# Up projection of the last feed-forward by a seven-product 2x2 scheme, on one Trainium2 core

## The chip, the core and the metric

One program runs on one core of a Trainium2 chip. The metric is the device time of one execution in microseconds. The kernel before takes 1809.07 us (median of 3 runs, 1808.6 to 1810.55). Engines are named as in the profile: PE is TensorE's matmul, PEld its weight load, DVE is VectorE, ACT is ScalarE, POOL is GpSimd, SP is SyncE, which issues most transfers.

## What is computed

A stream of 512 tokens with 1024 channels passes through two layers, each a SwiGLU feed-forward, a token mixer (Fourier, then convolution) and a second SwiGLU feed-forward, all modulated by a conditioning vector. The change lies in the last feed-forward alone:

```python
def swiglu(h, w_in, w_out):
    g, u = jnp.split(h @ w_in, 2, axis=-1)
    return (jax.nn.silu(g) * u) @ w_out
...
h = h + 0.5 * m[8] * swiglu(modulate(rms_norm(h), m[6], m[7]), w_ff_in[i, 1], w_ff_out[i, 1])
```

Here `w_in` is 1024 x 5632 and `w_out` 2816 x 1024, in fp32.

## The kernel before

Everything is kept with channels on the 128 partitions and the 512 tokens along the free axis. A product in fp32 is made of three matmuls on operands split in two: each operand is written as a rounded part (`_hi`) plus a remainder (`_lo`), and `product` (L1488) adds hi x hi, lo x hi and hi x lo in one PSUM bank. ACT makes every `_hi` by a copy into the rounded type, and DVE makes every `_lo` by subtracting it from the full value.

A feed-forward `f` goes through `NI = 11` steps. A step takes 256 gate columns and 256 up columns of `w_in`, that is two chunks `ch` of 128 gate and 128 up channels. For each chunk `up` (L1594) runs 8 blocks of input channels x 2 (gate, up) x 3 matmuls of 512 tokens into banks `ps[2*ch]` (gate) and `ps[2*ch+1]` (up). ACT takes the SiLU of the gate bank into `tmp_a` (`silu`, L779), DVE multiplies it with the up bank into `tmp_b` (`gate_product`, L1138), ACT and DVE split the result into `p_hi` and `p_lo` (L784, L1143). `down` (L1602) multiplies the step's two product chunks with 256 rows of `w_out` for 8 output chunks `d`, 6 matmuls each, in banks 4 to 7 in turn, and DVE adds each to the stream `h` (`flush`, L1148), times a gate. The down product of step `i - 1` runs behind the up products of step `i`:

```python
def step(i, par):
    up(f, i, 0)
    up(f, i, 1)
    down(f, i - 1, 1 - par)
```

Step 0 is `first_two` (L1533), which works on halves of 256 tokens while the normalised input is still being made. Steps 1 to 10 have the form above: step 1 by itself, 2 to 9 as a loop of four rounds of two steps (`LOOP_STEPS`, L68), 10 by itself. After step 10 the last down product (48 matmuls) runs and the output is stored.

Weights come in by SP: a pair (gate and up columns of one step, 2 MB, one of two buffers `raw_pair`) and a down block (1 MB, `raw_down`). ACT and DVE convert a chunk's pair in one instruction each of 128x2048 elements (`next_hi` L788, `next_lo` L1161), the down block likewise (L653, `down_lo` L985), into three weight buffers `w_hi`/`w_lo`, two for the up chunks and one for down. SP's `ff_step` (L465) waits until the second chunk of the pair two steps back is converted, loads the next pair into its place, then waits until the down block is converted and loads the next. Each engine's instructions run in the order in which they are written out, per engine, for each step: DVE's `ff_step` (L1165) does the down weights, the first chunk's product, its next weights, the second chunk's product, the eight flushes and the second chunk's next weights. Semaphore counts in the loops are computed from the loop register.

Before the last feed-forward, the norm (number 6) fills `a_hi` and `a_lo` half by half: DVE scales `h` into a temporary (`half_tmp`, L248, tiles of `tmp_b` and `tmp_c`), ACT adds the shift and rounds (`half_hi`, L708), DVE takes the remainder (`half_lo`, L1076). `y_conv` (L219) is a view of `raw_mod`, which is not used any more by then. POOL has no work in the last feed-forward.

Of the kernel before, what the change touches and what calls it, by code (L numbers as in the profile page):

```python
# [39 lines left out]
def hybrid_backbone(nc, x_chunks, c, w_mod, w_mod_first, w_ff_in, w_ff_out, fnet_w_out, conv_w_in, conv_w_out,  # L40
# [125 lines left out]
    with ctx:  # L166
# [229 lines left out]
        def _(sp):  # L396
# [90 lines left out]
            def feed_forward(f, next_pairs):  # L487
# [27 lines left out]
                with sp.Fori(0, LOOP_STEPS[f]) as r:  # L515
                    for odd in range(2):
                        step(r * 2 + (1 + odd), odd, f < 3)
                for i in range(1 + 2 * LOOP_STEPS[f], NI - 2):
                    step(i, (i - 1) % 2, i < UNIT_STEPS[f])
# [1430 lines left out]
```

## Time and profile before

| | us |
|---|---|
| median of 3 runs | 1809.07 |
| lowest, highest | 1808.6, 1810.55 |
| the profiled execution | 1811.04 |
| its span, first to last instruction | 1809.3 |
| PE busy | 1774.1 (98%) |
| DVE busy | 1112.4 (61%) |
| ACT busy | 600.8 (33%) |
| POOL busy | 170.9 (9%) |

The mean granted clock of TensorE is 0.991 of 2.4 GHz. A line of the page such as `L1579 PE MATMUL bank<-a_hi,w_hi 128*128 128x512 f32 x1408` names the line of the kernel, the engine, the tiles and the shape. "Busy" of one instruction runs from its start to its end, and on every engine the next instruction may start before that end, so that the distance between starts (here called the pitch) is read from the timeline. Steps 1 to 10 of the last feed-forward lie at 1468.46 to 1794.86 us of the span.

### The profile page before, as it was taken

What the parts mean: (1) busy time and instruction counts of PE and PEld (TensorE: products, weight loads), DVE (VectorE), ACT (ScalarE), POOL (GpSimd) and SP (SyncE); (2) the same over time, 40 slices, a digit from 0 to 9 for tenths busy, and PEclk for the clock granted to TensorE, in tenths of its full rate; (3) what the DMA queues carried; (4) which work ended last, traced back from release to release, by engine and by line L of the source; (5) the groups of instructions that cost most, each with busy time, mean ns of one, the idle gap of its engine ahead of it and who ended that gap; (6) DMA issues with size and microseconds to landing.
All of it is one profiled execution on the core that took longest, in us unless ns stands there. A gap on an engine that the chain in (4) does not pass through costs nothing.

```text
span 1809.3 us, 21295 instructions
## 1 busy us (share of the span) xinstructions
PE 1774.1 (98%) x8424; PEld 1470.6 (81%) x8424; DVE 1112.4 (61%) x1448; ACT 600.8 (33%) x761; POOL 170.9 (9%) x146
## 2 busy tenths in 40 slices
PE   7999999999999999999999999999999999999999
PEld 5788888889888888888988888888765888888887
DVE  5865665667766656566656556456898555444454
ACT  5422222235342222223422222226676442222221
POOL 0000000020300000001000000004994200000000
PEclk8999999999999999999999999999999999999999
DMA  9744353330633534534343535221211322423301
GB/s 370 285 159 190 116 205 143 142 137 1 227 145 116 216 132 150 198 116 148 108 165 144 204 116 183 72 70 48 93 48 47 117 71 70 139 70 104 105 23 70
DMA packets 133375, 238.07 MB, mean 132 GB/s; under 512 B 3777, under 2 KB 110401, under 8 KB 124738
## 3 DMA queue, kind: packets, MB, share of 16 engines
q1 hardware_dynamic: 133168, 236.99, 36.5%
q8 instruction: 42, 0.69, 0.2%
q10 hardware_dynamic: 146, 0.24, 0.0%
q14 instruction: 19, 0.16, 0.0%
HBM read 235.12 MB, written 2.10 MB: 131 GB/s over the span
## 4 chain that ended last, share of the span: by engine, by line
PE 88%; DVE 4%; POOL 4%; ACT 2%; issue 1%; DMA 0%; POOLq 0%; ACTq 0%; DVEq 0%
PE bank L1584 16%; PE bank L1579 16%; PE bank L1580 16%; PE bank L1490 10%; PE bank L1492 10%; PE bank L1491 10%; POOL tmp_c L628 3%; PE bank L1804 2%; PE bank L1526 1%; PE bank L1528 1%; PE bank L1530 1%; POOL sq_sum L593 1%; DVE w_lo L972 1%; ACT raw_down L934 1%; DVE bank L1450 1%
## 5 line engine op out<-in xcount | busy, mean ns | idle before, releaser
L1579 PE MATMUL bank<-a_hi,w_hi 128*128 128x512 f32 x1408 | 551.7, 392 | 7.6 <-ACT a_hi L667 6.1
L1580 PE MATMUL bank<-a_hi,w_lo 128*128 128x512 f32 x1408 | 548.8, 390 | 0.0
L1584 PE MATMUL bank<-a_lo,w_hi 128*128 128x512 f32 x1408 | 433.5, 389 | 2.2 <-DVE a_lo L1315 2.2
L1151 DVE SCALAR_TENSOR_TENSOR h<-bank,half_gate,h 128x512 f32<-128x512 f32 x328 | 242.3, 749 | 128.7 <-PE bank L1492 126.7
L1579 PEld LDWEIGHTS bank<-a_hi,w_hi 128*128 128x128 f32 x1408 | 264.8, 188 | 64.5 <-issue 7.6
L1584 PEld LDWEIGHTS bank<-a_lo,w_hi 128*128 128x128 f32 x1408 | 264.5, 188 | 58.0 <-DVE a_lo L1315 3.1
L1580 PEld LDWEIGHTS bank<-a_hi,w_lo 128*128 128x128 f32 x1408 | 264.8, 188 | 56.4 <-issue 1.4
L1490 PE MATMUL bank<-p_hi,w_hi 128*128 128x512 f32 (+1 forms) x752 | 285.5, 380 | 2.2 <-DVE h L1158 1.7
L1491 PE MATMUL bank<-p_hi,w_lo 128*128 128x512 f32 (+1 forms) x752 | 283.9, 378 | 0.0
L1492 PE MATMUL bank<-p_lo,w_hi 128*128 128x512 f32 (+1 forms) x752 | 283.9, 377 | 0.0
L1141 DVE TENSOR_TENSOR tmp_b<-tmp_a,bank 128x512 f32<-128x512 f32 x88 | 60.5, 688 | 333.6 <-ACT tmp_a L782 333.6
L782 ACT ACTIVATE tmp_a<-bank 128x512 f32<-128x512 f32 x88 | 52.8, 600 | 632.6 <-PE bank L1584 622.0
L972 DVE TENSOR_TENSOR w_lo<-raw_pair,w_hi 128x2048 fp32r<-128x2048 f32 x100 | 230.5, 2306 | 49.5 <-ACT w_hi L794 46.8
L653 ACT ACTIVATE w_hi<-raw_down 128x2048 fp32r<-128x2048 f32 x44 | 84.4, 1919 | 261.9 <-PE bank L1492 257.4
L1490 PEld LDWEIGHTS bank<-p_hi,w_hi 128*128 128x128 f32 x752 | 143.1, 190 | 29.8 <-DVE h L1158 4.0
L1491 PEld LDWEIGHTS bank<-p_hi,w_lo 128*128 128x128 f32 x752 | 143.1, 190 | 25.8
L1492 PEld LDWEIGHTS bank<-p_lo,w_hi 128*128 128x128 f32 x752 | 143.1, 190 | 25.4
L993 DVE SCALAR_TENSOR_TENSOR raw_mod<-raw_mod,silu_b 128x1024 f32<-128x1024 f32 x132 | 154.5, 1224 | 0.0
L794 ACT ACTIVATE w_hi<-raw_pair 128x2048 fp32r<-128x2048 f32 x80 | 152.3, 1903 | 0.0
L588 POOL TENSOR_TENSOR sq_sum<-tmp_a 128x256 f32<-128x256 f32 x10 | 9.3, 935 | 1204.2 <-ACT tmp_a L701 1204.2
L988 DVE TENSOR_TENSOR w_lo<-raw_down,w_hi 128x2048 fp32r<-128x2048 f32 x44 | 100.6, 2287 | 9.3 <-ACT w_hi L653 9.2
L628 POOL TENSOR_TENSOR tmp_c<-tmp_c,raw_down 128x512 f32<-128x512 f32 x67 | 97.8, 1460 | 9.6
(177 smaller groups left out, 1669.6 us busy)
## 6 DMA issues: line engine op xcount, KB each, us to landing
raw_pair<-in_w_ff_in SPq DMA_DIRECT2D x86, 1024.0 KB, 7.5
raw_mod<-mod_blocks SPq DMA_DIRECT2D x66, 1024.0 KB, 8.9
raw_down<-in_w_ff_out SPq DMA_DIRECT2D x44, 1024.0 KB, 8.6
raw_pair<-in_conv_w_in SPq DMA_DIRECT2D x8, 1024.0 KB, 6.8
raw_pair<-in_fnet_w_out SPq DMA_DIRECT2D x4, 1024.0 KB, 6.5
raw_pair<-in_conv_w_out SPq DMA_DIRECT2D x4, 1024.0 KB, 6.5
h<-x_chunks SPq DMA_DIRECT2D x4, 512.0 KB, 6.1
raw_pair<-mod_first SPq DMA_DIRECT2D x2, 1024.0 KB, 10.3
```

What stands on the lines that cost most here:

```text
L628: pool.tensor_tensor(acc, acc, pool_term[:, term % TERMS], ALU.add).then_inc(s_pool_tap, 1)
L794: act.activation(w_hi[b][:], raw_pair[pair % 2][:, :, ch, :], ACT.Copy).then_inc(s_w_hi[b], 1)
L972: dve.tensor_tensor(w_lo[b][:], raw_pair[pair % 2][:, :, j, :], w_hi[b][:].bitcast(F32), ALU.subtract).then_inc(s_w[b], 1)
L988: dve.tensor_tensor(w_lo[b][:], raw_down[:], w_hi[b][:].bitcast(F32), ALU.subtract).then_inc(s_w[b], 1)
L993: dve.scalar_tensor_tensor(out=block, in0=block, scalar=1.0, in1=silu_b[:], op0=ALU.mult, op1=ALU.mult, accum_out=mod_dot[:, column]).then ...
L1151: dve.scalar_tensor_tensor(out=h[:, d], in0=ps[4 + d % 4][:], scalar=half_gate[:, f, d:d + 1], in1=h[:, d], op0=ALU.mult, op1=ALU.add).the ...
L1490: pe.matmul(bank, wh, xh, start=start, stop=False, skip_group_check=True)
L1491: pe.matmul(bank, wl, xh, start=False, stop=False, skip_group_check=True)
L1492: return pe.matmul(bank, wh, xl, start=False, stop=stop, skip_group_check=True)
L1579: pe.matmul(ps[bank][:], tile_hi, a_hi[:, k], start=k == 0, stop=False, skip_group_check=True)
L1580: pe.matmul(ps[bank][:], tile_lo, a_hi[:, k], start=False, stop=False, skip_group_check=True)
L1584: ins = pe.matmul(ps[bank][:], w_hi[b[bank // 2]][:, bank % 2 * KD + k], a_lo[:, k], start=False, stop=k == KD - 1, skip_group_check=True)
```

## The change

From step 2 on, the up projection of the last feed-forward is computed as a 2x2 block product with seven block products instead of eight. Per chunk the weight is cut into A11, A12 (gate columns, input channels 0-511 and 512-1023) and A21, A22 (up columns), the input into B11, B12, B21, B22 (input channel halves by token halves). Sums of weights S1 to S4 are made for every step, sums of the input T1 to T4 once, and the seven products X are added up as they come. Each block product ("piece") is 4 blocks of channels x 3 matmuls of 256 tokens, 12 matmuls.

- PE: `fast_step` runs 14 pieces (7 for each chunk), each behind its own waits, and then `down` as before. Steps 2 to 10 use it, step 1 keeps the old form.
- ACT: the pair is converted in 14 instructions of 128x512 (`piece_hi`), the down weights in 4 of 128x512; 6 copies of 128x256 take partial sums out of PSUM (`partial_copy`); SiLU now reads `tmp_a` in SBUF.
- DVE: 14 instructions of 128x512 for the pieces' remainders (`piece_lo`), 8 of 128x512 for the weight sums (`weight_sum`, partly in place in the raw pair), 4 for the down remainders, 4 + 2 additions of 128x256 with PSUM (`gate_sum`, `up_sum`), the product in two halves of 128x256 (`fast_product`), and flushes and `product_lo` as before, in an order written out by hand.
- In step 1 DVE and ACT also make T1 to T4 and their parts (`moving_sums`, `moving_sum_hi`, `moving_sum_lo`), the first pieces and sums for step 2 (`step_before_fast`); norm 6 keeps its temporaries in `y_conv`. The functions `step_before_fast` of ACT, `piece_lo`, `moving_sum_lo` (128x1024 each), `down_lo_part` and the forms for step 10 are left out below; in step 10 the remainders of the last down block stand between flushes 1 and 2.
- Weight pieces use the two up buffers as a ring of 8 places: piece m + 8 waits until PE has used piece m.
- SP loads pair i + 2 when the last piece of step i is converted (before: when the second chunk of step i was, during step i - 1).

```diff
+    FAST = 3
+    FAST_FROM = 2
+    FAST_NORM = 6
+    PIECES = [(0, "A11"), (0, "A12"), (1, "A11"), (1, "A12"), (0, "S2"), (0, "S1"), (1, "S2"), (1, "S1"), (0, "S3"),
+      (0, "S4"), (1, "S3"), (1, "S4"), (0, "A22"), (1, "A22")]
+    NPC = len(PIECES)
+    SLOTS = 8
+    PRODUCTS = {"A11": ("B11", "a", True), "A12": ("B21", "b", True), "S2": ("T2", "a", False),
+        "S1": ("T1", "c", True), "S3": ("T3", "a", False), "S4": ("B22", "c", False),
+        "A22": ("T4", "a", False)}
+    COPIES = [(0, "X1"), (1, "X1"), (0, "X2"), (0, "X5"), (1, "X2"), (1, "X5")]
+    SUMS = [(0, "S3"), (0, "S1"), (1, "S3"), (1, "S1"), (0, "S2"), (1, "S2"), (0, "S4"), (1, "S4")]
+    T_ORDER = ["T2", "T1", "T3", "T4"]
...
     UP[f] = FIRST[ph]
+    standard = 1 if f == FAST else NI - 1
+    place(x_, standard), place(y_, standard)
...
-def half_tmp(k):
+def half_tmp(k, n):
+    if n == FAST_NORM:
+        return y_conv[:, k]
...
+def half_bank(ch, name):
+    return ps[2 * ch + (name != "a")][:, 0:HT]
+t_place = {"T1": (0, 0), "T2": (1, 1), "T3": (0, 1), "T4": (1, 0)}
+t_full = {name: quarter(y_conv, *at) for name, at in t_place.items()}
+t_hi = {"T1": t1_hi_in_silu[:], "T2": t2_hi_in_u[:], "T3": quarter(a_hi, 0, 1), "T4": quarter(a_lo, 0, 1)}
+moving_hi = dict(t_hi, B11=quarter(a_hi, 0, 0), B21=quarter(a_hi, 1, 0), B22=quarter(a_hi, 1, 1))
+moving_lo = {name: quarter(t_lo_in_mod, *at) for name, at in t_place.items()}
+moving_lo.update(B11=quarter(a_lo, 0, 0), B21=quarter(a_lo, 1, 0), B22=quarter(a_lo, 1, 1))
...
+def piece_tiles(w, m):
+    b = UP[FAST][m % SLOTS // 4][0]
+    return w[b][:, 4 * (m % 4):4 * (m % 4 + 1)]
+def raw_quarter(slot, ch, name):
+    n = ("A11", "A12", "A21", "A22").index(name)
+    return raw_pair[slot][:, 4 * n:4 * (n + 1), ch, :]
+def piece_raw(slot, ch, name):
+    if name == "S3":
+        return tap_last[:] if ch == 0 else taps_extra[:].rearrange("p (k n) -> p k n", n=P)
+    return raw_quarter(slot, ch, {"S1": "A21", "S2": "A11", "S4": "A12"}.get(name, name))
...
-            sp.wait_ge(s_w[UP[f][1][0]], i + (UP[f][1][1] + 1))
+            if f == FAST and not (isinstance(i, int) and i < FAST_FROM):
+                sp.wait_ge(s_piece, piece_no(i, NPC - 1))
+            else:
+                sp.wait_ge(s_w[UP[f][1][0]], i + (UP[f][1][1] + 1))
...
+    def piece_hi(i, m, par):
+        ch, name = PIECES[m]
+        slot = (PAIR[FFD] + par) % 2
+        if m >= SLOTS:
+            act.wait_ge(s_used, piece_no(i, m - SLOTS))
+        elif not (isinstance(i, int) and i == FAST_FROM):
+            act.wait_ge(s_used, piece_no(i, (m + SLOTS if m + SLOTS < NPC else m) - NPC))
+        if name[0] == "S":
+            act.wait_ge(s_sum, sum_no(i, ch, name))
+        act.activation(piece_tiles(w_hi, m), piece_raw(slot, ch, name), ACT.Copy).then_inc(s_piece_hi, 1)
+    def partial_copy(i, ch, name):
+        m = PIECES.index((ch, {"X1": "A11", "X2": "S2", "X5": "S1"}[name]))
+        act.wait_ge(s_used, piece_no(i, m))
+        src = half_bank(ch, "c" if name == "X5" else "a")
+        dst = {"X1": tmp_a[:, ch, HALF[0]], "X2": tmp_a[:, ch, HALF[1]], "X5": tmp_b[:, ch, HALF[1]]}[name]
+        act.activation(dst, src, ACT.Copy).then_inc(s_copied, 1)
...
+    def fast_silu(i, ch):
+        act.wait_ge(s_gate_sum, i * 4 + (ch + 3 - 4 * FAST_FROM))
+        act.activation(tmp_a[:, ch], tmp_a[:, ch], ACT.Silu).then_inc(s_silu, 1)
...
+    def fast_step(i, par):
+        f = FAST
+        last = isinstance(i, int) and i == NI - 1
+        act.wait_ge(s_take, i * KD + (HB[FFD] - KD))
+        down = (DOWN[f][0], i * 16 + 16 * TAIL[FFD])
+        partial_copy(i, 0, "X1")
+        piece_hi(i, 8, par)
+        piece_hi(i, 9, par)
+        partial_copy(i, 1, "X1")
+        piece_hi(i, 10, par)
+        piece_hi(i, 11, par)
+        down_hi_part(*down, 0)
+        partial_copy(i, 0, "X2")
+        piece_hi(i, 12, par)
+        partial_copy(i, 0, "X5")
+        piece_hi(i, 13, par)
+        down_hi_part(*down, 1)
+        partial_copy(i, 1, "X2")
+        down_hi_part(*down, 2)
+        partial_copy(i, 1, "X5")
+        down_hi_part(*down, 3)
...
+        next_pair_loaded(i, par)
+        piece_hi(i + 1, 0, 1 - par)
+        fast_silu(i, 0)
+        piece_hi(i + 1, 1, 1 - par)
+        piece_hi(i + 1, 2, 1 - par)
+        fast_silu(i, 1)
+        piece_hi(i + 1, 3, 1 - par)
+        piece_hi(i + 1, 4, 1 - par)
+        product_hi(f, i, 0, par)
+        for m in (5, 6):
+            piece_hi(i + 1, m, 1 - par)
+        product_hi(f, i, 1, par)
+        piece_hi(i + 1, 7, 1 - par)
...
+    def weight_sum(i, ch, name, par):
+        slot = (PAIR[FFD] + par) % 2
+        raw = {q: raw_quarter(slot, ch, q) for q in ("A11", "A12", "A21", "A22")}
+        if name == "S3":
+            if not (isinstance(i, int) and i == FAST_FROM):
+                dve.wait_ge(s_piece, piece_no(i, PIECES.index((ch, "S3")) - NPC))
+            x, y, op = raw["A11"], raw["A21"], ALU.subtract
+        elif name == "S1":
+            dve.wait_ge(s_sum, sum_no(i, ch, "S3"))
+            x, y, op = raw["A21"], raw["A22"], ALU.add
+        elif name == "S2":
+            dve.wait_ge(s_sum, sum_no(i, ch, "S1"))
+            dve.wait_ge(s_piece, piece_no(i, PIECES.index((ch, "A11"))))
+            x, y, op = raw["A21"], raw["A11"], ALU.subtract
+        else:
+            dve.wait_ge(s_sum, sum_no(i, ch, "S2"))
+            dve.wait_ge(s_piece, piece_no(i, PIECES.index((ch, "A12"))))
+            x, y, op = raw["A12"], raw["A11"], ALU.subtract
+        dve.tensor_tensor(piece_raw(slot, ch, name), x, y, op).then_inc(s_sum, 1)
...
+    def moving_sums(layer, v):
+        shift = mod[:, layer, v * KD:(v + 1) * KD]
+        dve.tensor_tensor(shift_step, shift[:, 4:8], shift[:, 0:4], ALU.subtract).then_inc(s_t_sum, 1)
+        dve.tensor_tensor(t_full["T1"], quarter(y_conv, 0, 1), quarter(y_conv, 0, 0),
+                          ALU.subtract).then_inc(s_t_sum, 1)
+        dve.wait_ge(s_t_sum, 2)
+        for k in range(4):
+            dve.scalar_tensor_tensor(out=t_full["T3"][:, k], in0=y_conv[:, 4 + k, HALF[1]],
+                                     scalar=shift_step[:, k:k + 1], in1=y_conv[:, k, HALF[1]], op0=ALU.add,
+                                     op1=ALU.subtract).then_inc(s_t_sum, 1)
...
+    def gate_sum(i, ch, hf):
+        dve.wait_ge(s_copied, copy_no(i, ch, "X2" if hf else "X1"))
+        dve.wait_ge(s_used, piece_no(i, PIECES.index((ch, "S4" if hf else "A12"))))
+        part = tmp_a[:, ch, HALF[hf]]
+        dve.tensor_tensor(part, half_bank(ch, "c" if hf else "b"), part, ALU.add).then_inc(s_gate_sum, 1)
+    def up_sum(i, ch):
+        dve.wait_ge(s_copied, copy_no(i, ch, "X5"))
+        dve.wait_ge(s_used, piece_no(i, PIECES.index((ch, "S3"))))
+        part = tmp_b[:, ch, HALF[1]]
+        dve.tensor_tensor(part, half_bank(ch, "a"), part, ALU.add).then_inc(s_up_sum, 1)
+    def fast_product(i, ch):
+        dve.wait_ge(s_silu, i * 2 + (2 * NI * FAST + ch + 1))
+        dve.wait_ge(s_up_sum, pair_count(i, ch + 1))
+        dve.wait_ge(s_used, piece_no(i, PIECES.index((ch, "A22"))))
+        dve.tensor_tensor(tmp_b[:, ch, HALF[1]], tmp_a[:, ch, HALF[1]], tmp_b[:, ch, HALF[1]], ALU.mult)
+        dve.tensor_tensor(tmp_b[:, ch, HALF[0]], tmp_a[:, ch, HALF[0]], half_bank(ch, "a"),
+                          ALU.mult).then_inc(s_prod, 1)
...
+    def step_before_fast():
+        f = FAST
+        down_lo((DOWN[f][0], 1 + (DOWN[f][1] - 1)))
+        moving_sums(1, 6)
+        gated(f, 1, 0, 1)
+        moving_sum_lo("T2")
+        moving_sum_lo("T1")
+        i, par = FAST_FROM, FAST_FROM % 2
+        next_pair_loaded(1, 1)
+        weight_sum(i, 0, "S3", par)
+        weight_sum(i, 0, "S1", par)
+        piece_lo(i, 0, par)
+        weight_sum(i, 1, "S3", par)
+        weight_sum(i, 1, "S1", par)
+        piece_lo(i, 1, par)
+        weight_sum(i, 0, "S2", par)
+        piece_lo(i, 2, par)
+        weight_sum(i, 1, "S2", par)
+        piece_lo(i, 3, par)
+        gated(f, 1, 1, 1)
+        flush(f, 0, 0)
+        moving_sum_lo("T3")
+        flush(f, 0, 1)
+        moving_sum_lo("T4")
+        for n in range(4):
+            flush(f, 0, 2 + n)
+            piece_lo(i, 4 + n, par)
+        flush(f, 0, 6)
+        weight_sum(i, 0, "S4", par)
+        flush(f, 0, 7)
+        weight_sum(i, 1, "S4", par)
...
+    def fast_step(i, par):
+        f = FAST
+        last = isinstance(i, int) and i == NI - 1
+        down = (DOWN[f][0], i + (DOWN[f][1] - 1))
+        piece_lo(i, 8, par)
+        gate_sum(i, 0, 0)
+        piece_lo(i, 9, par)
+        gate_sum(i, 1, 0)
+        piece_lo(i, 10, par)
+        piece_lo(i, 11, par)
+        down_lo_part(down, 0)
+        piece_lo(i, 12, par)
+        piece_lo(i, 13, par)
+        down_lo_part(down, 1)
...
+        next_pair_loaded(i, par)
+        weight_sum(i + 1, 0, "S3", 1 - par)
+        weight_sum(i + 1, 0, "S1", 1 - par)
+        down_lo_part(down, 2)
+        weight_sum(i + 1, 1, "S3", 1 - par)
+        weight_sum(i + 1, 1, "S1", 1 - par)
+        down_lo_part(down, 3)
+        up_sum(i, 0)
+        piece_lo(i + 1, 0, 1 - par)
+        gate_sum(i, 0, 1)
+        weight_sum(i + 1, 0, "S2", 1 - par)
+        up_sum(i, 1)
+        piece_lo(i + 1, 1, 1 - par)
+        piece_lo(i + 1, 2, 1 - par)
+        gate_sum(i, 1, 1)
+        weight_sum(i + 1, 1, "S2", 1 - par)
+        piece_lo(i + 1, 3, 1 - par)
+        fast_product(i, 0)
+        piece_lo(i + 1, 4, 1 - par)
+        fast_product(i, 1)
+        flush(f, i - 1, 0)
+        product_lo(f, i, 0, par)
+        piece_lo(i + 1, 5, 1 - par)
+        flush(f, i - 1, 1)
+        piece_lo(i + 1, 6, 1 - par)
+        flush(f, i - 1, 2)
+        product_lo(f, i, 1, par)
+        flush(f, i - 1, 3)
+        piece_lo(i + 1, 7, 1 - par)
+        flush(f, i - 1, 4)
+        weight_sum(i + 1, 0, "S4", 1 - par)
+        flush(f, i - 1, 5)
+        weight_sum(i + 1, 1, "S4", 1 - par)
+        flush(f, i - 1, 6)
+        flush(f, i - 1, 7)
...
+    def fast_step(i, par):
+        for m, (ch, name) in enumerate(PIECES):
+            x, bank, first = PRODUCTS[name]
+            pe.wait_ge(s_piece, piece_no(i, m))
+            if name == "A11":
+                pe.wait_ge(s_prod, i * 2 + (2 * NI * FAST + ch - 1))
+            elif name == "S1":
+                pe.wait_ge(s_gate_sum, i * 4 + (ch + 1 - 4 * FAST_FROM))
+            elif name == "S2":
+                pe.wait_ge(s_copied, copy_no(i, ch, "X1"))
+            elif name == "S3":
+                pe.wait_ge(s_copied, copy_no(i, ch, "X2"))
+            elif name == "S4":
+                pe.wait_ge(s_copied, copy_no(i, ch, "X5"))
+            elif name == "A22":
+                pe.wait_ge(s_up_sum, pair_count(i, ch + 1))
+            hi, lo = piece_tiles(w_hi, m), piece_tiles(w_lo, m)
+            for k in range(KD // 2):
+                ins = product(half_bank(ch, bank), hi[:, k], lo[:, k], moving_hi[x][:, k], moving_lo[x][:, k],
+                              first and k == 0, k == KD // 2 - 1)
+            ins.then_inc(s_used, 1)
+        down(FAST, i - 1, 1 - par)
...
         step(1, 1)
+        if f == FAST:
+            pe.wait_ge(s_t_lo, len(T_ORDER))
+            step = fast_step
```

## Rows read from the trace of the kernel before

**Rows 1.** The page: busy time by engine, and the chain's shares by engine.

```profile
PE 1774.1 (98%) x8424; PEld 1470.6 (81%) x8424; DVE 1112.4 (61%) x1448; ACT 600.8 (33%) x761; POOL 170.9 (9%) x146
PE 88%; DVE 4%; POOL 4%; ACT 2%; issue 1%; DMA 0%; POOLq 0%; ACTq 0%; DVEq 0%
```

**Rows 2.** Busy time by stretch: step 1, step 2 and step 10; columns as named.

```profile
core 0: us, PE busy (x) PEld busy (x) DVE busy (x) ACT busy (x) POOL busy (x), PEclk, DMA share, GB/s
1468.46:1501.10 32.64, 32.64 (x144) 27.03 (x145) 16.64 (x18) 10.46 (x10) 0.00 (x0) 1.00 0.28 97
1501.10:1533.74 32.64, 32.64 (x146) 27.03 (x145) 15.28 (x15) 8.00 (x7) 0.00 (x0) 1.00 0.29 97
1762.22:1794.86 32.64, 32.64 (x146) 27.03 (x145) 15.28 (x15) 6.19 (x6) 0.00 (x0) 1.00 0.10 33
```

**Rows 3.** Timeline of PE in a loop step, 512 columns: start, busy us.

```profile
1718.84 0.39 PE L1490 MATMUL bank<-p_hi,w_hi 128*128 128x512 f32 x1
...
1719.52 0.39 PE L1490 MATMUL bank<-p_hi,w_hi 128*128 128x512 f32 x1
```

**Rows 4.** Timeline of PE before step 0, 256 columns, to a boundary with waits.

```profile
1442.14 0.28 PE L1491 MATMUL bank<-a_hi,w_lo 128*128 128x256 f32 x1
...
1443.21 0.28 PE L1491 MATMUL bank<-a_hi,w_lo 128*128 128x256 f32 x1
1443.33 0.29 PE L1492 MATMUL bank<-a_lo,w_hi 128*128 128x256 f32 x1
1443.46 0.29 PE L1528 MATMUL bank<-a_hi,w_hi 128*128 128x256 f32 x1
1443.59 0.28 PE L1530 MATMUL bank<-a_hi,w_lo 128*128 128x256 f32 x1
1443.70 0.28 PE L1528 MATMUL bank<-a_hi,w_hi 128*128 128x256 f32 x1
```

**Rows 5.** Timeline of DVE, neighbours without idle time: 512, flush, 2048, 256 elements.

```profile
1468.33 0.69 DVE L1145 TENSOR_TENSOR p_lo<-tmp_b,p_hi 128x512 fp32r<-128x512 f32 x1
1468.93 0.68 DVE L1141 TENSOR_TENSOR tmp_b<-tmp_a,bank 128x512 f32<-128x512 f32 x1
...
1697.28 0.75 DVE L1151 SCALAR_TENSOR_TENSOR h<-bank,half_gate,h 128x512 f32<-128x512 f32 x1 [0.61 <-PE bank L1492]
1697.95 2.28 DVE L972 TENSOR_TENSOR w_lo<-raw_pair,w_hi 128x2048 fp32r<-128x2048 f32 x1
1700.15 2.29 DVE L988 TENSOR_TENSOR w_lo<-raw_down,w_hi 128x2048 fp32r<-128x2048 f32 x1
...
1455.07 0.48 DVE L1072 SCALAR_TENSOR_TENSOR tmp_c<-h,mod,bank 128x256 f32<-128x256 f32 x1
1455.46 0.48 DVE L1080 SCALAR_TENSOR_TENSOR a_lo<-tmp_b,mod,a_hi 128x256 fp32r<-128x256 f32 x1
```

**Rows 6.** Timeline of DVE: L1462 waits for L1457, the instruction just before it.

```profile
1332.19 0.69 DVE L1457 TENSOR_TENSOR raw_mod<-raw_mod,bank 128x512 f32<-128x512 f32 x1
1332.91 0.70 DVE L1462 TENSOR_TENSOR bank<-bank,raw_mod 128x512 f32<-128x512 f32 x1
```

**Rows 7.** Timeline of ACT, then the group of a 128x256 copy from PSUM.

```profile
1709.51 0.63 ACT L786 ACTIVATE p_hi<-tmp_b 128x512 fp32r<-128x512 f32 x1 [0.76 <-DVE tmp_b L1141]
1710.05 1.90 ACT L794 ACTIVATE w_hi<-raw_pair 128x2048 fp32r<-128x2048 f32 x1
...
L741 ACT ACTIVATE sq_sum<-bank 128x256 f32<-128x256 f32 x2 | 0.8, 380 | 1.0 <-PE bank L1519 1.0
```

**Rows 8.** DMA issues in 1480 to 1809 us: KB each, us to landing.

```profile
raw_pair<-in_w_ff_in SPq DMA_DIRECT2D x14, 1024.0 KB, 6.4
raw_down<-in_w_ff_out SPq DMA_DIRECT2D x9, 1024.0 KB, 8.5
```

**Rows 9.** Timeline of DVE in step 1: the first down weights.

```profile
1474.53 2.29 DVE L988 TENSOR_TENSOR w_lo<-raw_down,w_hi 128x2048 fp32r<-128x2048 f32 x1
```

**Rows 10.** Instruction queue in 1480 to 1809 us (packets, MB); PE's waits.

```profile
q8 instruction: 5, 0.08, 0.1%
...
PE bank L1804 <- issue: 2.3, 1, 2.3
```

More of the change, by code:

```diff
@@ L189, in hybrid_backbone @@
         raw_down = sb("raw_down", [P, 16, P])
+        with nc.sbuf_tensor("t_lo_in_mod", [P, KD, T], F32R) as t_lo_in_mod:
+            pass
         raw_mod = sb("raw_mod", [P, 2, 4, MU])
@@ L192, in hybrid_backbone @@
         mod_dot = sb("mod_dot", [P, 2 * NV * KD])
+        with nc.sbuf_tensor("t1_hi_in_silu", [P, KD // 2, T // 2], F32R) as t1_hi_in_silu:
+            pass
         silu_b = sb("silu_b", [P, D])
@@ L197, in hybrid_backbone @@
         sq_sum = sb("sq_sum", [P, T])
+        with nc.sbuf_tensor("t2_hi_in_u", [P, KD // 2, T // 2], F32R) as t2_hi_in_u:
+            pass
         u_pad = sb("u_pad", [P, 3, T + 2 * HALO])
@@ L513, in step @@
                         ff_step(f, i, None, 0, 0, load_up)
[L515 to L519, printed above, removed]
+                if f == FAST:
+                    step(1, 0, False)
+                    with sp.Fori(0, LOOP_STEPS[f] - 1) as r:
+                        for odd in range(2):
+                            step(r * 2 + (2 + odd), 1 - odd, False)
+                    step(NI - 3, 1, False)
+                else:
+                    with sp.Fori(0, LOOP_STEPS[f]) as r:
+                        for odd in range(2):
+                            step(r * 2 + (1 + odd), odd, f < 3)
+                    for i in range(1 + 2 * LOOP_STEPS[f], NI - 2):
+                        step(i, (i - 1) % 2, i < UNIT_STEPS[f])
                 for n, i in enumerate((NI - 2, NI - 1)):
@@ new lines, in fast_silu, with down_hi_part @@
+            def fast_silu(i, ch):
+                act.wait_ge(s_gate_sum, i * 4 + (ch + 3 - 4 * FAST_FROM))
+                act.activation(tmp_a[:, ch], tmp_a[:, ch], ACT.Silu).then_inc(s_silu, 1)
+            def down_hi_part(b, loads, n):
+                act.wait_ge(s_down_in, loads)
+                rows = slice(4 * n, 4 * n + 4)
+                ins = act.activation(w_hi[b][:, rows], raw_down[:, rows], ACT.Copy)
+                if n == 3:
+                    ins.then_inc(s_w_hi[b], 1)
@@ L824, in step @@
                     ff_step(f, i, par, isinstance(i, int) and i == NI - 1, next_unit)
+                if f == FAST:
+                    step_before_fast()
+                    with act.Fori(0, LOOP_STEPS[f]) as r:
+                        for odd in range(2):
+                            fast_step(r * 2 + (2 + odd), odd)
+                    fast_step(NI - 1, (NI - 1) % 2)
+                    return
                 step(1, 1)
@@ L1227, in step @@
                             next_unit, after_down)
+                if f == FAST:
+                    step_before_fast()
+                    with dve.Fori(0, LOOP_STEPS[f]) as r:
+                        for odd in range(2):
+                            fast_step(r * 2 + (2 + odd), odd)
+                    fast_step(NI - 1, (NI - 1) % 2)
+                    return
                 step(1, 1, f < 3, gate_columns if f == 0 else None)
```

109 lines of the change are left out of this document (105 added, 4 removed).

## The prediction

> **What bounds the kernel now.** I read the page first: PE is busy 98% of the span, and the chain that ended last lies on PE for 88% [rows 1]. Then the table by stretch, over the part that changes: in steps 1, 2 and 10 alike PE is busy for all of 32.64 us at clock 1.00, which is 2.4 GHz, while DVE has 15 to 17 us of work, ACT 6 to 10 and POOL none [rows 2]. Nothing ever holds PE there, so a step is worth what its matmuls cost, and it stays so until another engine needs the step's whole time. Last the timelines, for what one instruction occupies of its engine, since the busy times overlap. PE: three matmuls of 512 columns from 1718.84 to 1719.52, 0.2267 us each [rows 3], and 144 x 0.2267 = 32.64. At 256 columns, with a new weight for each, nine from 1442.14 to 1443.21, 0.119; I use 0.120 [rows 4].
>
> **PE, the term that pays.** A step's up projection falls from 96 matmuls of 512 columns (21.76 us) to 14 pieces x 12 = 168 of 256 columns, 168 x 0.120 = 20.16 us. Down stays at 48 x 0.2267 = 10.88. The step goes from 32.64 to 31.04, 1.60 less, and steps 2 to 10 are nine: 14.40 us. Seven products for eight would give an eighth, 2.72 us, if time went with columns; 1.12 of it is lost because a matmul costs about 13 ns above its columns at 2.4 GHz (213.3 and 106.7 ns) and there are 72 more of them.
> The Trainium skill (TensorE: Matmul & The Clock Gate, Back-to-back issue gap) has 2.5 ns in place of these 13, which would make it 144 x 215.8 against 168 x 109.2 + 48 x 215.8 ns, an estimate of 2.37 us a step or 21.3 in all. The rows say 0.2267 and 0.120, and they decide.
>
> **PE's waits.** Each piece has one to three waits whose counts come from the loop register. If they are met early they cost little: at a boundary with three waits two pitches of 0.13 stand for 0.12, 20 ns together [rows 4]. Those are constants, so I bound a piece by 0 and 30 ns and take 10, nearer to that row per wait: 14 x 9 x 0.010 = 1.26 us (0 to 3.8).
>
> **DVE, the cover.** Pitches: 128x512 0.60, flush 0.67, 128x2048 2.20 [rows 5]. The slope between 512 and 2048 gives 0.33 for 128x256 (a three-operand one has 0.39 [rows 5]) and 1.13 for 128x1024. A step now holds 14 remainders, 8 weight sums, 4 down remainders, 2 product remainders, 28 x 0.60 = 16.8; 8 flushes, 5.4; 10 halves (4 + 2 sums, 4 products), 3.3. S1 waits for S3 right in front of it: such a pair starts 0.72 apart where 0.60 is the pitch [rows 6], so 2 x 0.12. Sum 25.7 of 31.04 us: it fits, if not much is lost by waiting. ACT has 22 instructions of 512 at 0.54 [rows 7] and six copies of 256 from PSUM (0.38 busy [rows 7], some 0.30 apart): 13.7 us.
>
> **The order, laid out against PE** (us after the first piece starts; piece m ends at 1.44(m + 1), and its result is seen 0.16 to 0.2 later, as busy exceeds pitch). Piece 8's place comes free when piece 0 is used: ACT copies X1 and rounds piece 8, so DVE can begin its remainder at 2.6. Up to the remainder of piece 13 (9.8 to 10.4) DVE follows ACT, which follows PE, one place per 1.44, and idles some 4 us. From there it runs almost without a break: sums S3 and S1, down remainders, `up_sum`, next pieces, products, flushes. PE's wants, and when they are met: piece 5 wants the first gate half at 7.2 (met 3.6); piece 12 wants the first up half at 17.28 (15.2); piece 13 the second at 18.72 (17.1); down chunk 4 wants flush 0 at 25.6 (23.6); chunk 5 flush 1 at 26.96 (25.4); chunk 6 flush 2 at 28.3 (26.7); chunk 7 flush 3 at 29.7 (28.0). Flush 7 ends 1.4 into the next step, where the first remainder cannot start before 2.6 anyway. So PE is never held, with 1.5 us to spare at the tightest want and 1.2 at the wrap.
>
> **Step 1 pays.** DVE's first down remainder starts 6.07 after the step [rows 9]. It takes 2.2, and behind it now stand the input sums (some 0.2 + 1.13 + 0.12 + 12 x 0.395 = 6.2), the remainders of T2 and T1 (2.3, behind ACT's two of 128x1024), four weight sums S3 and S1 (2.6), two S2 (1.2), four piece remainders (2.4) and both products, each 0.69, then ACT's 0.63 [rows 7], then 0.60 and signals (4.0). That is 27.0, and 0.4 more for waiting on ACT: flush 0 starts at 27.4, where down chunk 4 wants it done at 27.2; remainders T3 and T4 stand between flushes 0 to 2. PE loses 1.0, 0.45 and 0.45 at chunks 4 to 6, 1.9 us. Bounds: 0 and 4.5 (the latter with 0.09 more per DVE instruction). DVE enters step 2 some 4.3 us late and just makes the first gate half.
>
> **What costs nothing.** SP loads a pair once the last piece is converted, at 10.4, instead of in the step before; two of 1 MB land some 6.4 us after issue [rows 8], and the next sums want them 31 us later. The down load queued behind it on SP starts at 14.8, lands by about 24 (8.5 [rows 8]), wanted at 37.5. In step 10 the last down block lands at about 22.3, and its split is done at 26.5; PE wants it at 31. Cover gone, each of these would hold PE for what it is late. Norm 6 writes the same shapes to another tile, and POOL's queue has nothing. After step 10 the work is unchanged.
>
> **Sum.** -14.40 + 1.9 + 1.26 = -11.24. The profiled execution took 1811.04, so 1799.8 for it; the median stands 1.97 lower, 1797.8.
>
> **Rivals.** B: DVE's pitch here is its busy time (0.69 for 0.60, 0.42 for 0.33), because nearly every instruction has waits on registers in front of it. With 0.09 more on each, the layout gives step 1 at 37.15 and steps of 31.50 with the piece term, -5.8: 1803.3. Against it, flushes and remainders behind register waits keep the short pitch [rows 5]; for it, up to three waits in front of one instruction is more than any row has. The Trainium skill (VectorE: DVE Perf Modes, The DRAIN you can't avoid) says that the next operation does not start until the pipe is empty, which speaks for B; the starts in [rows 5] lie 0.08 to 0.09 before the ends, against it.
> C, slower: DVE becomes the bound. From 0.12 more on each instruction (the self-wait of [rows 6]) the layout gains nothing; at 0.15 flushes 0 to 3 come late, PE stands before down chunks 4 to 7 in every step, a step takes 32.95 to 33.0, step 1 39.0, and the sum is +9.2: 1818.2. For it: the chain PE, ACT, DVE, PE is new in the step and repeats for every piece. Against it: the layout has every want met 1.5 us early.
> D: PE's loop body grows from 288 to 432 matmuls and their weight loads, and each branch back has to fetch. Today it does not: five instruction packets served the whole stretch [rows 10]. PE once stood 2.3 us for nothing the profile shows, elsewhere [rows 10]; three branches back at that price are 6.9 us: -4.3, 1804.7. The Trainium skill (Runtime: NRT & Kernel Launch, Instruction fetch mechanics) gives PE 2048 instructions, room for the new body, yet also says that a branch beyond two pages stalls; today's body of 576 matmuls and loads is already longer than two of its pages of 256, and [rows 10] show no fetch.
> E: the 13 ns shrink with the columns, so that 256 columns cost half of 0.2267. Then a step is 29.92, and the sum -24.5 + 3.2: 1787.8. [Rows 4] speak against it. The gap formula of the Trainium skill (TensorE: Matmul & The Clock Gate, Back-to-back issue gap), with its smaller constant, leans that way.
>
> **Chances.** Forecast 0.60, B 0.20, C 0.11, D 0.05, E 0.02, and 0.02 for B and D together, no change. About 0.2% (3.6 us) is what a measurement of this kernel can tell from no change. The forecast's own bounds are -12.5 and -6.5 (pieces at 30 ns, 0.05 more on DVE); no stall in step 1 and free waits give -14.4. The range takes in that, B and D: 1794.5 to 1806, and leaves out C, E and the rest. Faster: forecast, most of B and D, E: 0.81; same 0.08; slower 0.11.
>
> **What would show it.** By stretch, steps of some 31.2 us with PE busy throughout and DVE near 29.5 of busy time; 256-column pitch of 0.120 within a piece, and at most 0.01 to 0.03 more at its start; the waits of PE naming `h` (flush) in step 1 only. B: DVE starts no earlier than the end in front. C: PE idle before down chunks 4 to 7, released by flushes, in every step. D: PE idle at every second step's start, with more instruction packets. A steady stall before a piece, released by a remainder or a PSUM copy, would make the layout wrong.

## The result and the profile after

The changed kernel takes 1820.16 us (median of 4 runs, 1819.25 to 1823.7) where the kernel before takes 1808.91 beside it: a ratio of 1.0065, 95% interval 1.0053 to 1.0077. It is 11 us slower; 11 us less was forecast. The profiled execution took 1819.44, its span is 1817.7.

The page of the changed kernel, busy time and the chain's shares by engine; it answers to [rows 1]:

```profile
PE 1764.2 (97%) x9072; PEld 1490.3 (82%) x9072; DVE 1219.8 (67%) x1745; ACT 662.0 (36%) x954; POOL 170.8 (9%) x146
...
PE 82%; DVE 9%; POOL 4%; ACT 3%; issue 2%; DMA 0%; DVEq 0%; ACTq 0%; POOLq 0%
```

PE has 9.9 us less to do, but the chain that ended last now lies on DVE for 9% where it was 4%. The table by stretch says where (steps 1, 2, 6 and 10 of the changed kernel; it answers to [rows 2]):

```profile
core 0: us, PE busy (x) PEld busy (x) DVE busy (x) ACT busy (x) POOL busy (x), PEclk, DMA share, GB/s
1465.94:1500.59 34.65, 33.64 (x144) 26.90 (x145) 30.94 (x46) 14.81 (x20) 0.00 (x0) 1.00 0.27 92
1500.59:1534.33 33.74, 31.59 (x218) 29.12 (x216) 27.32 (x49) 14.43 (x28) 0.00 (x0) 1.00 0.28 94
1635.51:1670.23 34.72, 32.75 (x217) 30.66 (x216) 27.07 (x49) 14.42 (x28) 0.00 (x0) 0.95 0.26 91
...
1772.39:1803.38 30.99, 30.99 (x217) 29.11 (x216) 20.90 (x35) 11.95 (x21) 0.00 (x0) 1.00 0.11 35
```

Step 10 takes what was forecast for every fast step, 30.99 us with PE busy throughout. Six of the steps 2 to 9 take 33.73 on average, with some 2.1 us in which PE stands; steps 6 and 8 take 34.72 and 34.71 and show a clock of 0.95. Step 1 takes 34.65. Before, it took 32.78 and not 32.64: the stretches of [rows 2] are cut 32.64 long, and the first matmul of step 2 starts at 1501.24, 0.14 later than the first of them ends.

```profile
1468.46:1501.24 32.78, 32.78 (x144) 27.14 (x145) 16.64 (x18) 10.46 (x10) 0.00 (x0) 1.00 0.28 97
```

What PE and DVE waited for in the changed kernel, from step 1 on (us in total, times, longest):

```profile
PE bank L1883 <- DVE tmp_b L1455: 16.8, 14, 2.0
PE bank L1883 <- DVE h L1342: 0.7, 1, 0.7
...
DVE w_lo L1470 <- ACT w_hi L929: 44.9, 9, 5.0
```

`tmp_b` at L1455 is `up_sum`, for which piece 12 (chunk 0) and piece 13 (chunk 1) wait: eight times before piece 12, and six before piece 13, as the two steps with the lower clock don't have the second wait. And DVE, said to run without a break by then, stands 5.0 us in each of the nine fast steps in front of `down_lo_part` (L1470). The timeline of step 6 of the changed kernel, whose first piece starts at 1635.51, DVE first (start, busy us, in brackets the idle time before):

```profile
1641.80 0.68 DVE L1388 TENSOR_TENSOR w_lo<-taps_extra,w_hi 128x512 fp32r<-128x512 f32 x1
1642.40 0.68 DVE L1388 TENSOR_TENSOR w_lo<-raw_pair,w_hi 128x512 fp32r<-128x512 f32 x1
1648.11 0.69 DVE L1470 TENSOR_TENSOR w_lo<-raw_down,w_hi 128x512 fp32r<-128x512 f32 x1 [5.02 <-ACT w_hi L929]
...
1654.39 0.42 DVE L1455 TENSOR_TENSOR tmp_b<-bank,tmp_b 128x256 f32<-128x256 f32 x1
```

The same step on ACT, where L929 is the conversion of one of the four parts of the down weights:

```profile
1642.08 0.61 ACT L929 ACTIVATE w_hi<-raw_down 128x512 fp32r<-128x512 f32 x1
...
1645.12 0.62 ACT L929 ACTIVATE w_hi<-raw_down 128x512 fp32r<-128x512 f32 x1
1645.74 0.39 ACT L916 ACTIVATE tmp_a<-bank 128x256 f32<-128x256 f32 x1
1646.03 0.62 ACT L929 ACTIVATE w_hi<-raw_down 128x512 fp32r<-128x512 f32 x1
1647.17 0.38 ACT L916 ACTIVATE tmp_b<-bank 128x256 f32<-128x256 f32 x1 [0.52 <-PE bank L1885]
1647.45 0.62 ACT L929 ACTIVATE w_hi<-raw_down 128x512 fp32r<-128x512 f32 x1
```

Part 0 is converted at 1642.69, in time for a remainder at 1643.0. The remainder starts at 1648.11, when part 3 is done (1648.07). The code says why, in two functions that the diff ahead of the prediction leaves out:

```python
# ACT, down_hi_part
ins = act.activation(w_hi[b][:, rows], raw_down[:, rows], ACT.Copy)
if n == 3:
    ins.then_inc(s_w_hi[b], 1)
# DVE, down_lo_part
dve.wait_ge(s_w_hi[b], use + 1)
```

The conversion is cut into four, but its count is still one for the whole block. So the remainder of part 0, placed between those of pieces 11 and 12, waits for part 3. That conversion stands on ACT behind the copy of chunk 1's X5, which PE's piece 7 releases 11.66 after the step's start. All that is behind it on DVE, down to `up_sum`, is late.

On PE, in the same step, the end of piece 11 and the start of piece 12:

```profile
1652.61 0.28 PE L1885 MATMUL bank<-a_lo,w_hi 128*128 128x256 f32 x1
1654.86 0.48 PE L1883 MATMUL bank<-a_lo,w_hi 128*128 128x256 f32 x1 [1.97 <-DVE tmp_b L1455]
1655.13 0.42 PE L1884 MATMUL bank<-a_lo,w_lo 128*128 128x256 f32 x1
...
1656.20 0.41 PE L1883 MATMUL bank<-a_lo,w_hi 128*128 128x256 f32 x1
1656.41 0.41 PE L1884 MATMUL bank<-a_lo,w_lo 128*128 128x256 f32 x1
...
1658.61 0.28 PE L1883 MATMUL bank<-a_lo,w_hi 128*128 128x256 f32 x1
1658.73 0.28 PE L1884 MATMUL bank<-a_lo,w_lo 128*128 128x256 f32 x1
```

From 1652.61 to 1654.86 are 2.25 us where 0.12 is the pitch. Then the pitch is 0.21, and back at 0.12 from 1658.5 on: in this step the clock fell behind the stall.

The account, from the first matmul of step 1 to the last matmul of the kernel: 1468.46 to 1805.65 before, 1465.94 to 1814.05 after, 10.9 us more. The pieces save 14.7 (nine steps of 31.01 for 32.64). Against that stand 1.9 for step 1, 21.8 for the stalls (8 steps of 33.73 for 31.01) and 2.0 for the lower clock in two steps: -14.7 + 1.9 + 21.8 + 2.0 = +11.0. (The spans differ by only 8.4 because step 1 starts 2.5 us earlier in this execution. What lies ahead of it varies: over the profiles of this study step 1 starts between 1463.5 and 1468.5.)

### The profile page after: what moved, and what is told of

Read it like the earlier page. It is cut to its first block, busy times and chain, and to the rows that moved or that the text cites. A ratio compares the mean times of both kernels' runs of the same rounds, so it can differ in the third digit from the quotient of the medians.

```text
span 1817.7 us, 23826 instructions
## 1 busy us (share of the span) xinstructions
PE 1764.2 (97%) x9072; PEld 1490.3 (82%) x9072; DVE 1219.8 (67%) x1745; ACT 662.0 (36%) x954; POOL 170.8 (9%) x146
## 4 chain that ended last, share of the span: by engine, by line
PE 82%; DVE 9%; POOL 4%; ACT 3%; issue 2%; DMA 0%; DVEq 0%; ACTq 0%; POOLq 0%
PE bank L1883 13%; PE bank L1885 12%; PE bank L1884 12%; PE bank L1977 12%; PE bank L1972 12%; PE bank L1973 12%; POOL tmp_c L712 3%; PE bank L2225 1%; PE bank L1919 1%; PE bank L1921 1%; PE bank L1923 1%; DVE w_lo L1388 1%; DVE w_lo L1470 1%; DVE w_lo L1163 1%; POOL sq_sum L677 1%
## 5 line engine op out<-in xcount | busy, mean ns | idle before, releaser
L1972 PE MATMUL bank<-a_hi,w_hi 128*128 128x512 f32 x1120 | 439.6, 393 | 7.3 <-ACT a_hi L751 5.8
L1973 PE MATMUL bank<-a_hi,w_lo 128*128 128x512 f32 x1120 | 436.8, 390 | 0.0
L1977 PE MATMUL bank<-a_lo,w_hi 128*128 128x512 f32 x1120 | 344.6, 389 | 2.4 <-DVE a_lo L1708 2.4
L1972 PEld LDWEIGHTS bank<-a_hi,w_hi 128*128 128x128 f32 x1120 | 210.8, 188 | 53.0 <-issue 7.3
L1977 PEld LDWEIGHTS bank<-a_lo,w_hi 128*128 128x128 f32 x1120 | 210.3, 188 | 47.0 <-DVE a_lo L1708 3.2
L1973 PEld LDWEIGHTS bank<-a_hi,w_lo 128*128 128x128 f32 x1120 | 210.8, 188 | 44.9 <-issue 1.4
L1163 DVE TENSOR_TENSOR w_lo<-raw_pair,w_hi 128x2048 fp32r<-128x2048 f32 x82 | 189.3, 2310 | 39.5 <-ACT w_hi L878 36.7
L1883 PE MATMUL bank<-a_hi,w_hi 128*128 128x256 f32 (+1 forms) x420 | 126.3, 301 | 0.0
L1884 PE MATMUL bank<-a_hi,w_lo 128*128 128x256 f32 (+1 forms) x420 | 126.1, 300 | 0.0
L878 ACT ACTIVATE w_hi<-raw_pair 128x2048 fp32r<-128x2048 f32 x62 | 118.0, 1903 | 0.0
## 6 DMA issues: line engine op xcount, KB each, us to landing
raw_pair<-mod_first SPq DMA_DIRECT2D x2, 1024.0 KB, 10.4
```

The costliest lines, as they stand in the source:

```text
L878: act.activation(w_hi[b][:], raw_pair[pair % 2][:, :, ch, :], ACT.Copy).then_inc(s_w_hi[b], 1)
L1163: dve.tensor_tensor(w_lo[b][:], raw_pair[pair % 2][:, :, j, :], w_hi[b][:].bitcast(F32), ALU.subtract).then_inc(s_w[b], 1)
L1883: pe.matmul(bank, wh, xh, start=start, stop=False, skip_group_check=True)
L1884: pe.matmul(bank, wl, xh, start=False, stop=False, skip_group_check=True)
L1972: pe.matmul(ps[bank][:], tile_hi, a_hi[:, k], start=k == 0, stop=False, skip_group_check=True)
L1973: pe.matmul(ps[bank][:], tile_lo, a_hi[:, k], start=False, stop=False, skip_group_check=True)
```

## The experiments

The theory: the one count for four parts is all that is wrong; without it the layout of the prediction holds. Rival 1: DVE has too much to do in this order, and the idle time would only move. Rival 2: ACT's chain is late by itself. All runs are of the changed kernel with the edits shown, in which `...` stands for lines left out.

**A count for each part** (e1_parts).

```diff
...
-                ins = act.activation(w_hi[b][:, rows], raw_down[:, rows], ACT.Copy)
-                if n == 3:
-                    ins.then_inc(s_w_hi[b], 1)
+                act.activation(w_hi[b][:, rows], raw_down[:, rows], ACT.Copy).then_inc(s_down_part, 1)
...
-                dve.wait_ge(s_w_hi[b], use + 1)
+                dve.wait_ge(s_down_part, i * 4 + (n + 1 - 4 * FAST_FROM))
```

> Each of ACT's four conversions of the down weights counts for itself, and the remainder of part n waits for conversion n alone; the order of all engines stays as in the changed kernel. Theory (the one count that stands for all four parts makes DVE idle 5.0 us in each step and so delays up_sum): DVE's idle time in front of the first down remainder falls from 5.0 us to under 1, PE no longer stands before piece 12 (it lost 2.13 of pitch there) and piece 13 (0.33), no step has matmuls at 1.2 GHz, steps 2 to 10 take 31.04, and the time is about 1796.5 us (1795.5 to 1798.5), 12 less than before. Rival 1 (DVE has too much to do in this order, the idle time only moves): the stall moves to another wait of PE, steps stay above 33, time 1808 or more. Rival 2 (ACT's own chain is late): DVE waits as long for a later part, PE stands before pieces 12 and 13 by 0.5 or more, time 1800 to 1808.

1797.79 us (6 runs, 1794.61 to 1800.13), 0.9932 of the kernel before, interval 0.9917 to 0.9946. The table by stretch of this kernel, steps 1, 2 and 10:

```profile
1468.08:1502.76 34.68, 33.69 (x145) 26.91 (x146) 30.97 (x46) 14.81 (x20) 0.00 (x0) 1.00 0.26 91
1502.76:1533.76 31.00, 31.00 (x217) 29.11 (x216) 28.71 (x52) 14.43 (x28) 0.00 (x0) 1.00 0.31 103
1750.81:1781.81 31.00, 31.00 (x217) 29.12 (x216) 20.14 (x33) 11.94 (x21) 0.00 (x0) 1.00 0.10 35
```

Its waits from step 1 on, PE's and DVE's own for the down parts:

```profile
PE bank L1882 <- DVE h L1341: 0.7, 1, 0.7
...
DVE w_lo L1469 <- ACT w_hi L930: 0.7, 1, 0.7
```

All nine fast steps take 31.00 or 31.01 with PE never held; what DVE waits for the down parts falls from 44.9 to 0.7 us in all. From the first matmul of step 1 to the last one it is 324.39 us against 337.19 before, 12.80 less, and 23.7 less than with the one count. The theory holds, and both rivals are out. The timeline of DVE in its step 6, whose first piece starts at 1626.78, shows the layout itself:

```profile
1634.28 0.68 DVE L1469 TENSOR_TENSOR w_lo<-raw_down,w_hi 128x512 fp32r<-128x512 f32 x1
...
1641.60 0.42 DVE L1454 TENSOR_TENSOR tmp_b<-bank,tmp_b 128x256 f32<-128x256 f32 x1
...
1643.46 0.42 DVE L1454 TENSOR_TENSOR tmp_b<-bank,tmp_b 128x256 f32<-128x256 f32 x1
...
1649.56 0.74 DVE L1341 SCALAR_TENSOR_TENSOR h<-bank,half_gate,h 128x512 f32<-128x512 f32 x1
```

The two up sums end 15.24 and 17.10 after the start, flush 0 at 23.52. The prediction had 15.2, 17.1 and 23.6.

**The one count kept, the remainders moved** (e2_order): all four down remainders stand together, where part 3 is done anyway (in step 10 behind the remainder of piece 13).

```diff
                 piece_lo(i, 11, par)
-                down_lo_part(down, 0)
                 piece_lo(i, 12, par)
                 piece_lo(i, 13, par)
-                down_lo_part(down, 1)
...
                 weight_sum(i + 1, 0, "S1", 1 - par)
-                down_lo_part(down, 2)
                 weight_sum(i + 1, 1, "S3", 1 - par)
                 weight_sum(i + 1, 1, "S1", 1 - par)
+                down_lo_part(down, 0)
+                down_lo_part(down, 1)
+                down_lo_part(down, 2)
                 down_lo_part(down, 3)
```

> The single count for the four down parts stays as in the changed kernel, but the four down remainders stand together behind the remainders of pieces 12 and 13 and the four sums S3 and S1, where the fourth conversion is done. Theory: same as with a count for each part, 1796.5 us (1795.5 to 1798.5), steps of 31.04, no stall before pieces 12 and 13. If the extra semaphore counts or the finer waits themselves were what helps, this one would stay at 1808 or more. Rival 1 (too much DVE work): 1808 or more here too. Rival 2 (ACT late): DVE stands in front of the first down remainder by 1 us or more again, and PE before piece 12: 1800 to 1808.

1796.95 us (1793.99 to 1799.49), 0.9929 (0.9914 to 0.9943); 324.38 from step 1 to the end, 12.81 less than before. Its step 2 in the table by stretch; steps 3 to 10 are like it:

```profile
1500.78:1531.79 31.01, 31.01 (x218) 29.12 (x217) 28.11 (x51) 14.43 (x28) 0.00 (x0) 1.00 0.31 103
```

It cannot be told from the kernel with four counts: what cost the time was the place of the wait in DVE's order together with its count, and mending either is enough. DVE's waits for the down parts, in all of this kernel, are one of 2.2 us in step 10, where nothing hangs on it:

```profile
DVE w_lo L1470 <- ACT w_hi L929: 2.2, 1, 2.2
```

**Step 1 in another order** (e3_step1; with a count for each part).

```diff
-                gated(f, 1, 1, 1)
+                gate_product(f, 1, 1)
                 flush(f, 0, 0)
-                moving_sum_lo("T3")
+                product_lo(f, 1, 1, 1)
                 flush(f, 0, 1)
+                flush(f, 0, 2)
+                moving_sum_lo("T3")
+                flush(f, 0, 3)
                 moving_sum_lo("T4")
-                for n in range(4):
-                    flush(f, 0, 2 + n)
-                    piece_lo(i, 4 + n, par)
-                flush(f, 0, 6)
+                piece_lo(i, 4, par)
+                for n in range(3):
+                    flush(f, 0, 4 + n)
+                    piece_lo(i, 5 + n, par)
```

> As with a count for each part, and DVE's order in step 1 changed: the first flush stands in front of the second chunk's product remainder, flush 1 behind that, flush 2 before the remainder of T3, flush 3 before that of T4, and the remainders of pieces 4 to 7 behind. Theory: of the 1.80 us that PE loses in step 1 (before the first products and down chunks 4 to 6) at most 0.5 stay, so 1.3 to 1.8 less than with the old order of step 1: about 1794.9 us (1794 to 1796.5). Rival: what is put off is wanted in step 2, and PE stands before its pieces 4 to 7 or the first gate half of step 2 by the same 1.3 to 1.8: no difference.

1796.69 us (1795.24 to 1799.15), 0.993 (0.9917 to 0.9943), just above the range expected. Steps 1 and 2 of this kernel in the table by stretch:

```profile
1467.88:1500.65 32.77, 32.77 (x144) 27.15 (x145) 29.72 (x44) 14.80 (x20) 0.00 (x0) 1.00 0.29 97
1500.65:1531.66 31.01, 31.01 (x217) 29.11 (x216) 29.79 (x54) 14.32 (x28) 0.00 (x0) 1.00 0.30 103
```

Step 1 falls from 34.68 to 32.77, and step 2 does not pay for it: 322.49 us from step 1 to the end, 14.70 less than before, which is all that the pieces save. The medians of the two kernels differ by 1.1 us only, which six runs spread over 3.9 and 5.5 us don't resolve; the 1.9 are the trace's. By the trace it is the shortest of the three mended versions; by the device times it can't be told from the other two. All three are faster than the kernel before and the changed kernel.

**How much time DVE has to spare** (e_pad2, e_pad4, e_pad6): further DVE instructions whose results nothing uses, with a count for each part.

```diff
                 down_lo_part(down, 3, i)
+                dve.tensor_tensor(sq_sum[:], h[:, 0], h[:, 0], ALU.mult)
+                dve.tensor_tensor(tmp_c[:, 0], h[:, 0], h[:, 0], ALU.mult)
+...
                 up_sum(i, 0)
```

> As with a count for each down part, plus two further VectorE instructions of 128x512 (0.60 us each, their results unused) in front of the first up_sum in each of steps 2 to 9. Theory (with the count mended, up_sum 0 is done 15.2 us after the step's first piece and up_sum 1 at 17.1, where pieces 12 and 13 want them at 17.28 and 18.72): 1.2 us fit into the spare time, steps stay at 31.00, PE waits for nothing, the time is that of the kernel without the pads within 0.3%. Rival (VectorE's 26 us of work already fill the step as its waits lie, rival C of the prediction): a step grows by up to 1.2, the time by up to 9.6.

> The same with four such instructions (2.4 us). Theory: up_sum 0 is done at 17.6 where 17.28 is wanted, up_sum 1 at 19.5, so PE stands before pieces 12 and 13 by some 0.45 each, steps 2 to 9 take 31.9 (31.5 to 32.2), 7 us more than without the pads, about 1804. If the spare time were smaller than the layout says, steps would take up to 33.4.

> The same with five instructions of 128x512 and one of 256 elements (3.33 us). Theory: up_sum 0 is done at 18.6, PE stands before piece 12 by 1.4 and before piece 13 by 0.4, steps 2 to 9 take 32.85 (32.5 to 33.2), 15 us more than without the pads, about 1812, that is slower than the kernel before. Of the clock: in the changed kernel it fell to 1.2 GHz behind two of eight stalls of 2.0 us; if the length of a stall decides, stalls of 1.4 leave it at 2.4 GHz; if not, some steps have pieces with a pitch of 0.21 and take about 1 us more.

One run each: 1796.09, 1802.06 and 1811.99 us, with 1807.42 for the kernel before beside them. Steps 2 to 9 take 31.01, 32.07 and 33.01 each: an eighth of these stretches, from the start of step 2 to the end of step 9, with two, four and six pads.

```profile
1500.34:1748.39 248.05, 248.05 (x1729) 232.91 (x1728) 220.91 (x388) 115.36 (x224) 0.00 (x0) 1.00 0.28 93
```

```profile
1498.22:1754.75 256.53, 252.59 (x1730) 233.11 (x1728) 229.78 (x403) 115.44 (x224) 0.00 (x0) 1.00 0.27 90
```

```profile
1500.88:1764.94 264.06, 252.65 (x1730) 233.14 (x1729) 237.34 (x419) 115.44 (x224) 0.00 (x0) 1.00 0.26 88
```

PE's waits for `up_sum`, with four pads and then with six:

```profile
PE bank L1886 <- DVE tmp_b L1454: 3.9, 16, 0.3
```

```profile
PE bank L1888 <- DVE tmp_b L1454: 11.4, 16, 1.3
```

With two pads there is no such wait. From 2.4 to 3.33 us of padding a step grows by 0.94, one for one. Carried back from there, the first 2.4 - 1.07 = 1.3 us would be free. That is an estimate, and rather low, since the 1.07 hold what a stall costs beyond its length (last section). In e1_parts itself the second up sum is done at 1643.88, and the first matmul of piece 13, which wants it, starts at 1645.44: 1.56 to spare, where 1.5 was forecast at the tightest point. What the runs show is that 1.2 us are free and 2.4 are not; with 2.4 and with 3.33, PE waits for DVE in each of steps 2 to 9. The granted clock stayed at 2.4 GHz in all of these steps.

**The changed kernel once more** (after_again).

> The changed kernel itself, a second look. Steps of 33.73, PE standing about 2 us before piece 12 in steps 2 to 9. The clock fell to 1.2 GHz behind the stalls of two steps in the first profile: if it is chance, another number of steps has it here, or other ones; if something in the program fixes it, the same two.

1820.35 us, with PE's waits for `up_sum` at 16.6 us in all (16.8 in the first profile). The steps with the lower clock are not the same, and three: 4, 6 and 9, where the first profile has 6 and 8. The table by stretch of this second profile, those three steps:

```profile
core 0: us, PE busy (x), PEclk, DMA share, GB/s
1567.96:1602.67 34.71, 32.74 (x217) 0.95 0.27 91
1636.41:1671.14 34.73, 32.76 (x217) 0.95 0.27 91
1738.60:1773.31 34.71, 32.74 (x218) 0.95 0.09 31
```

So it is not tied to a place in the program. What chooses the steps stays open.

## Why the prediction was wrong

**The step that failed** is "The order, laid out against PE", in the sentence "Up to the remainder of piece 13 (9.8 to 10.4) DVE follows ACT, which follows PE, one place per 1.44, and idles some 4 us. From there it runs almost without a break". It lets the remainder of down part 0, which stands between those of pieces 11 and 12, go as soon as ACT has converted part 0: else the remainder of piece 13 couldn't be over at 10.4, since part 3 is converted at 12.56 (1648.07 - 1635.51). Its wait is for part 3. In the trace that remainder starts 12.60 after the step's start (1648.11 - 1635.51), against 7.50 with a count for each part; `up_sum` 0 is done at 19.30 where 15.2 was forecast and 17.28 wanted. In place of 2.1 us early it comes 2.0 late, in each of eight steps. Step 10, with no next step's sums in front of `up_sum`, has the same 5.0 us of idle DVE and loses nothing. The prediction weighed PE's waits piece by piece, but listed none of DVE's with its count, and `down_lo_part` was taken for what its name says.

Step by step, the rest:

- *PE's gain.* 31.00 a step in e1_parts against 31.04, so 14.7 for nine steps against 14.40; the 14 pieces take 20.10, and 20.10 / 168 = 0.1196 for a matmul of 256 columns. The 13 ns above the columns stand. The Trainium skill (TensorE: Matmul & The Clock Gate, Back-to-back issue gap) has 2.5 ns for them, in a formula that it gives for a single matmul and not for a stream with weight loads. These steps do not agree with that figure.
- *PE's waits* were taken at 1.26 us; they are nothing. The 20.10 include all 14 boundaries. (A piece has one or two waits, not one to three.)
- *Step 1* was taken at 1.9; it lost 1.9 (34.65 for 32.78), at down chunks 4 to 6 as forecast: 1.00, 0.43 and 0.44 there, for 1.0, 0.45 and 0.45. e3_step1 takes all of it back (32.77).
- *DVE's cover.* Pitches as read: 0.60 or 0.61 in the DVE rows above (1641.80 to 1642.40). With the count mended the times of the layout are within 0.1 us, from the first remainder (2.57 for 2.6) to the end of flush 7 (1.33 into the next step for 1.4).
- *Rival B* is out with that: the starts lie 0.08 before the ends, also behind waits on registers. *Rival D* is out: PE never stands at the start of a fast step, in e1_parts no wait of PE is left behind step 1, and the changed kernel has nine instruction packets from 1480 us on (six on q8, three on q14) where [rows 10] have five, but none between 1548 and 1772, while the loop branches back three times. *Rival E* is out with the 31.00.
- *Rival C* came closest in its number (1818.2 for 1820.16) and not in its mechanism: PE stood before pieces 12 and 13, released by `up_sum`, and not before down chunks 4 to 7 released by flushes; and DVE was idle, not overloaded. That it came so near is luck. "A steady stall before a piece" was named as what would make the layout wrong, and that is what came, though released by `up_sum` and not, as named there, by a remainder or a PSUM copy.
- *The sum* of -11.24, with the piece term at zero -12.5, is what the same change gives once the count is mended: -12.80 in the trace, 1797.79 us for 1797.8 forecast. That these two agree so closely is luck: the six runs spread over 5.5 us, and the trace gains 1.6 more than the sum. The forecast was of that kernel, not of this one.

## What to carry to other kernels

When a producer is cut into parts so that a consumer can start early, look whether its semaphore was cut too, or put the consumer behind the last part: an order worked out from durations is only as good as the list of every wait with its exact count, also those in functions whose names look harmless. An engine that is busy for only 67% of the time can hold PE, if one in-order wait stands in front of what PE wants next; the waits view of that second engine shows it at once (44.9 us), and a few pads show about how much is to spare. A stall of PE may cost more than its length.
